# A layer norm behind the experts: its factor applied by the transposing product, its shift laid into PSUM first, the second token tile's sums in another order

## The chip, the cores and the metric

The kernel runs on one core of a Trainium2 chip. Its time is the device time of one execution in microseconds (us). The engines are named as in the profile: PE is TensorE (matmuls and transposes), PEld its weight loads, DVE VectorE, ACT ScalarE, POOL GpSimd, SP the engine that issues most DMAs. They run side by side and meet only in semaphores.

## The reference, cut to what matters

Two blocks stand one behind the other: two layers of mixer, norm, expert layer, norm (256 tokens of 1024 features), and then one recurrent/retention layer with a feed-forward part. The change touches what lies between an expert layer and the projection behind it:

```python
def layer_norm(x, g, b):
    mu = jnp.mean(xf, axis=-1, keepdims=True)
    var = jnp.mean(jnp.square(xf - mu), axis=-1, keepdims=True)
    y = (xf - mu) * lax.rsqrt(var + LN_EPS) * g + b

for i in range(DEPTH):                       # DEPTH = 2
    m = even_mixer(...) if i % 2 == 0 else odd_mixer(...)
    x = layer_norm(DN_ALPHA * x + m, ln1_g[i], ln1_b[i])
    f = hier_moe(x, ...)                     # 32 experts, the best two of one group
    x = layer_norm(DN_ALPHA * x + f, ln2_g[i], ln2_b[i])     # this norm

q, k, v = jnp.split(x @ w_qkv, 3, axis=-1)   # reads it behind the experts of layer 0
proj = rms_norm_2(x, norm1_gain) @ w_in      # reads it behind the experts of layer 1
```

## The kernel before, in words

Every engine has a program of its own, written out by hand in the order in which it runs; nothing is scheduled by rules. The 256 tokens are two tiles of 128 (t = 0, 1), the 1024 features eight columns of 128 (c = 0 to 7). The stretch that the change touches comes twice, once behind the experts of layer 0 and once behind those of layer 1. The two are called **junction 1** (592 to 612 us in the profile) and **junction 2** (1182 to 1205 us).

At a junction PE has added the last pair of experts into PSUM banks 0 to 3 (`scatter_by_half`, L1029). DVE takes the statistics of a tile (`expert_stats`, L1881 and L1885), ACT the root of the variance (`norm_root`, L1489), and DVE makes (x - mean) * gain by halves (`expert_center`, L1907), then the reciprocal of the root (L1865) and x * factor + shift over the whole tile (`norm_scale`, L1891). The shift is the second row of LNR, which holds gain and shift on all 128 partitions. Only then is X ready, and PE transposes its eight 128x128 blocks (`transposes_by_token`, L778) into two PSUM banks.

The projection behind it works with a split of each operand in a high part (rounded to fp32r) and a low part (what is left): high*high, high*low and low*high, called HH, HL and LH in `normed_and_first_chunk`. ACT copies the high part of the input out of the transposes' banks (`high_input`, L1466; with a gain per feature eight small ACTIVATEs per tile, L1469, at junction 2), DVE makes the low part (`low_input`, L1842, at junction 2 L1845). The weights come in quarter tiles of 128x1024: ACT makes the high part (`high_tiles`, L1597), POOL the low part (`low_tiles`, L666), and the first four of them belong to the first chunk of 512 columns. `normed_and_first_chunk` computes that chunk: 24 products per token tile (8 columns, three kinds; L798), then the next chunks follow in `split_project_t` (L916), which waits for `w_lo`, the count of low tiles. A high tile of the next chunk may be written when PE has used the same buffer (`w_used`).

`keep_clock` (L950) are products whose results nobody reads; PE runs them while it would wait. Before the change five of them stand ahead of the branch that leads around the overflow rounds of the experts (`pe.If(more > 0)`), and two behind the first tile's transposes. Products of plain f32 are two records each in the trace, each with a weight load of its own; transposes and fp32r products are one record.

At junction 2 ACT also takes squares of the finished X (`rms_root`, L1497 and L1501), and DVE makes a diagonal of its inverse roots (L2294) that PE sums by columns (L1322) ahead of the second chunk. In ACT's program `rms_root` stands between `high_input` of tile 1 and the first high tile of the second chunk.

## Time and profile before

| what | value |
|---|---|
| time, median of 3 runs | 1523.52 us (1520.9 to 1523.73) |
| time of the profiled execution | 1520.87 us |
| its span in the trace | 1519.1 us |
| granted TensorE clock over the span | 0.998 |
| PE busy | 1471.6 us, 97% |
| DVE, ACT, POOL busy | 552.5, 466.8, 153.8 us |
| chain that ended last, by engine | PE 87%, DMA 5%, DVE 4%, ACT 2% |
| HBM | 500.40 MB read, 330 GB/s over the span |

A row of the timeline gives start, duration, engine, line, operation, output and inputs, shape, and in brackets how long the engine sat idle before and what ended that. Rows of one kind that touch are merged ("x8"), so a pitch from one product to the next is read from two starts. A matmul's duration is longer than its pitch, since products overlap.

### The profile page before, as it was taken

The page shows a single profiled execution, that of the slowest core. Times are in us where ns is not written, and L with a number is a line of the kernel's source. Part 1 is how long each engine was busy: PE and PEld are TensorE (multiplying, and loading weights), DVE is VectorE, ACT ScalarE, POOL GpSimd, SP SyncE. Part 2 cuts the span into 40 slices and gives each one's busy share as a digit, 9 for nine tenths or more (in the row PEclk, how much of TensorE's full clock was granted, in tenths as well). Part 3 has the DMA queues.
Part 4 walks back from the last instruction along what each step waited for, and adds up shares of the span by engine and source line. Part 5 has one row for each costly group of instructions (what it writes and reads, how often), then busy time and mean ns, then how long its engine had stood idle before and what let it go on. Part 6 is the DMA issues. An engine that isn't in the chain of part 4 may idle for free.

```text
span 1519.1 us, 19195 instructions
## 1 busy us (share of the span) xinstructions
PE 1471.6 (97%) x7726; PEld 879.3 (58%) x7726; DVE 552.5 (36%) x1151; ACT 466.8 (31%) x819; POOL 153.8 (10%) x126
## 2 busy tenths in 40 slices
PE   8989999999999999999999999999999999999998
PEld 7755454544544444977544545445444786788886
DVE  6645111111111114037321111211111487688965
ACT  4541111111111113456111111111111561577654
POOL 0211000000000002953100000000000610001200
PEclk9999999999999999999999999999999999999999
DMA  8655999999999999835899999999999846464410
GB/s 300 249 222 221 373 424 427 428 428 427 428 426 428 428 423 398 301 145 238 330 411 426 428 426 428 427 428 428 428 426 409 322 177 220 168 214 174 170 53 28
DMA packets 76228, 502.68 MB, mean 331 GB/s; under 512 B 4720, under 2 KB 6000, under 8 KB 49136
## 3 DMA queue, kind: packets, MB, share of 16 engines
q1 hardware_dynamic: 75280, 495.18, 79.9%
q0 software_dynamic: 864, 6.29, 1.0%
q8 instruction: 64, 1.05, 0.3%
q14 instruction: 20, 0.16, 0.0%
HBM read 500.40 MB, written 1.05 MB: 330 GB/s over the span
## 4 chain that ended last, share of the span: by engine, by line
PE 87%; DMA 5%; DVE 4%; ACT 2%; issue 1%; SPq 1%; POOL 0%; DVEq 0%; ACTq 0%
PE bank L1057 26%; PE bank L1090 14%; PE bank L916 9%; PE bank L1003 7%; PE bank L1374 6%; DMA ring<-in_w_up 4%; PE bank L1402 4%; PE bank L863 4%; PE bank L1017 3%; PE bank L1376 3%; PE bank L882 1%; PE bank L950 1%; PE bank L798 1%; SPq L606 1%; PE bank L1072 1%
## 5 line engine op out<-in xcount | busy, mean ns | idle before, releaser
L1057 PE MATMUL bank<-ring,arena 128*64 128x512 f32 x1280 | 284.2, 599 | 12.0 <-issue 6.8
L1057 PEld LDWEIGHTS bank<-ring,arena 128*64 128x64 f32 x1280 | 94.4, 138 | 196.8 <-issue 192.7
L1057 PE MATMUL bank<-arena 128*64 128x512 f32 x576 | 168.3, 592 | 3.5 <-issue 3.5
L2037 DVE TENSOR_TENSOR arena<-arena,bank 128x512 f32<-128x512 f32 x32 | 22.0, 688 | 383.0 <-PE bank L1057 383.0
L1090 PE MATMUL bank<-ring,arena 128*64 128x512 f32 x640 | 141.7, 595 | 2.4 <-ACT arena L1556 2.4
L1374 PE MATMUL bank<-x_split,w_high 128*128 128x512 f32 (+1 forms) x408 | 139.1, 392 | 0.2 <-DVE x_split L1845 0.2
L1003 PEld LDWEIGHTS bank<-SEL,x_by_row 128*128 128x128 f32 x1024 | 116.7, 192 | 25.8 <-issue 24.3
L1003 PE MATMUL bank<-SEL,x_by_row 128*128 128x128 f32 x1024 | 122.8, 278 | 0.0
L2051 DVE SCALAR_TENSOR_TENSOR y_low<-bank,ST,y_high 128x512 fp32r<-128x512 f32 x64 | 48.1, 751 | 202.4 <-ACT y_high L1560 202.4
L1560 ACT ACTIVATE y_high<-bank,ST 128x512 fp32r<-128x512 f32 x64 | 44.0, 687 | 245.6 <-PE bank L1090 245.6
L1057 PEld LDWEIGHTS bank<-arena 128*64 128x64 f32 x576 | 55.3, 137 | 110.7 <-issue 110.7
L1376 PE MATMUL bank<-x_split,w_low 128*128 128x256 f32 (+1 forms) x408 | 111.8, 274 | 0.0
L2403 DVE TENSOR_TENSOR w_low<-ring,w_high 128x1024 fp32r<-128x1024 f32 x72 | 96.7, 1345 | 30.8 <-ACT w_high L1754 30.6
L1553 ACT COPY arena<-bank 128x512 f32<-128x512 f32 x30 | 17.6, 586 | 262.7 <-PE bank L1003 262.7
L1090 PEld LDWEIGHTS bank<-ring,arena 128*64 128x64 f32 x640 | 45.9, 137 | 84.3 <-issue 84.3
L658 POOL DMA_DIRECT2D LNR<-in_ln_rows x6 | 3.8, 631 | 879.2 <-PE bank L1003 828.6
L1374 PEld LDWEIGHTS bank<-x_split,w_high 128*128 128x128 f32 x408 | 76.7, 188 | 17.5 <-DVE x_split L1845 0.3
L1090 PE MATMUL bank<-arena 128*64 128x512 f32 x288 | 85.0, 595 | 0.0
L1057 PE MATMUL bank<-first_over_features,arena 128*64 128x512 f32 x192 | 84.5, 593 | 0.0
L1754 ACT CAST w_high<-ring 128x1024 fp32r<-128x1024 f32 x72 | 75.5, 1051 | 25.9 <-PE bank L1402 25.9
L1376 PEld LDWEIGHTS bank<-x_split,w_low 128*128 128x128 f32 x408 | 77.2, 189 | 0.2 <-issue 0.2
L1547 ACT ACTIVATE arena<-bank 128x512 f32<-128x512 f32 x32 | 19.1, 598 | 156.9 <-PE bank L1057 156.9
(352 smaller groups left out, 2247.3 us busy)
## 6 DMA issues: line engine op xcount, KB each, us to landing
ring<-in_w_gate SPq DMA_DIRECT2D x32, 2048.0 KB, 27.2
ring<-in_w_up SPq DMA_DIRECT2D x32, 2048.0 KB, 22.5
ring<-in_w_down SPq DMA_DIRECT2D x32, 2048.0 KB, 24.3
arena<-in_w_gate SPq DMA_DIRECT2D x18, 2048.0 KB, 24.2
arena<-in_w_up SPq DMA_DIRECT2D x18, 2048.0 KB, 24.5
arena<-in_w_down SPq DMA_DIRECT2D x18, 2048.0 KB, 25.9
ring<-in_ffn_up SPq DMA_DIRECT2D x12, 2048.0 KB, 8.8
ring<-in_w_in SPq DMA_DIRECT2D x8, 2048.0 KB, 13.6
```

The lines of the kernel that those rows point to most:

```text
L863: last = nc.tensor.matmul(bank[(g0 + n) % 2 * 2 + t][:, :], tile(c, t), slot(i[n], C, 512)[:, c, :], start=(c == first), stop=(c == final))
L916: last = nc.tensor.matmul(part_(bank[g % 2 * 2 + t]), a, b, start=(part_ is parts[0] and c == 0 and n == 0), stop=(part_ is parts[-1] and ...
L1003: last = nc.tensor.matmul(bank[6 + c // 4][:, c % 4 * P:(c % 4 + 1) * P], x_rows(t, c), SEL[:, t, :], start=(t == 0), stop=(t == T - 1))
L1017: last = nc.tensor.matmul(bank[2 * t + half][:, :], SWT[:, t, :], y[:, 512 * half:512 * half + 512], start=False, stop=False, skip_group_c ...
L1057: last = nc.tensor.matmul(bank[4 + m][64 * e:64 * e + 64, :], XG[:, c, 64 * e:64 * e + 64], w[e][:, c, :], start=(c == 0), stop=(c == C - 1))
L1090: last = nc.tensor.matmul(bank[6 + half][64 * e:64 * e + 64, :], HT[:, j, 64 * e:64 * e + 64], w[e][:, j, 512 * half:512 * half + 512], st ...
L1374: nc.tensor.matmul(bank[f % 4][:, :].rearrange("p (a b) -> p a b", a=2)[:, :, a:b], WHI[f % WBUF][:, c, :], XSPLIT[:, :, c, a:b], start=(a ...
L1376: last = nc.tensor.matmul(bank[f % 4][:, a:b], WLO[f % WBUF][:, c, :], XHI[:, c, a:b], start=False, stop=(b == SEQ and c == C - 1), skip_g ...
L1402: last = nc.tensor.matmul(bank[4 + 2 * t + half][:, :], a, w.rearrange("p a b -> p (a b)"), start=(c == 0 and n == 0), stop=(c == DOWN_T - ...
L1754: nc.scalar.copy(WHI[k % WBUF][:, :, :], src).then_inc(w_hi, 1)
L2051: v.scalar_tensor_tensor(YLO[:, cols_], bank[6 + half][:, :], slot_gate, YHI[:, cols_].bitcast(F32), ALU.mult, ALU.subtract).then_inc(s["y ...
L2403: v.tensor_tensor(WLO[k % WBUF][:, :, :], ffn_weights(k)[1], WHI[k % WBUF][:, :, :], ALU.subtract)\
```

## The change

The factor 1/sqrt(var) of a token no longer has to be in X before the transposes. A transpose is a product with the identity; with a diagonal matrix in its place the same product scales each token as it transposes. ACT makes that matrix (`make_diagonal`: identity times the token's factor) in the buffer of SELW, which is free by then. The shift, which is a number per feature, is laid into the same PSUM blocks first by a product of LNR's second row with the first column of the identity, repeated 128 times (`shift_by_token`); `scaled_transposes` then adds onto it. Both are plain f32 products, where the transposes were moves.

X itself is finished by DVE later, behind both `low_input`s. The reciprocal stands between the two halves of `expert_center`. POOL no longer waits for X before its first low tile, and ACT begins with a high tile ahead of the first root. PE has two `keep_clock` products ahead of the branch and none behind it, and the sums of tile 1 are reordered: HH and HL of the first two weight tiles, then their LH, then the same for tiles 2 and 3.

```diff
         SEL, SELW = sb("SEL", [P, T, 2 * SLOTS]), sb("SELW", [P, T, 2 * SLOTS])
+        NORM_DIAG = SELW
         bank = [ctx.enter_context(nc.psum_tensor(f"bank{i}", [P, 512], F32)) for i in range(8)]
...
+        x_prepared, diag_made = sem("x_prepared"), sem("norm_diagonal_made")
...
             next_norm_rows(0, 1)
-            pool.wait_ge(x_ready, 3)
             low_tiles(S_QKV, range(3 * TILES))
             pool.wait_ge(x_ready, 4)
...
             next_norm_rows(1, 3)
-            pool.wait_ge(x_ready, 7)
             low_tiles(S_IN2, range(3 * TILES))
...
-            def normed_and_first_chunk(name, source, ready, n0, s, after):
+            def normed_and_first_chunk(name, l, s):
 
                 g, width = s["g0"], s["widths"][0]
                 HH, HL, LH = (XHI, 0), (XHI, 1), (XLO, 0)
@@ -798,15 +798,41 @@
                             last = nc.tensor.matmul(bank[g % 2 * 2 + t][:, 0:width], x[:, c, t * P:(t + 1) * P],
                                                     s["bufs"][q][half][:, c % 2, 0:width],
                                                     start=(kind is HH and c == 0),
-                                                    stop=(c == C - 1 and kind is kinds[-1] and kind is not HH and
-                                                          (t == 1 or kind is HL)))
+                                                    stop=(c == C - 1 and kind is (LH if t else HL)))
                     return last
 
                 def x_high(t, half):
                     pe.wait_ge((tr_act, tr_dve)[half], TR[name][0] // 2 + t + 1)
 
-                transposes_by_token(name, source, ready, n0, [0])
-                keep_clock(7, after)
+                def norm_blocks(t):
+
+                    for h in range(2):
+                        k = TR[name][0] + 2 * t + h
+                        pe.wait_ge(tr_dve if k % 2 else tr_act, (k - 4) // 2 + 1)
+                        for j in range(4):
+                            c = 4 * h + j
+                            yield h, j, bank[4 + k % 4][:, j * P:(j + 1) * P], slice(c * P, (c + 1) * P)
+
+                def shift_by_token(t):
+
+                    pe.wait_ge(ln_loaded, 16 * (2 * l + 2))
+                    for h, j, block, features in norm_blocks(t):
+                        nc.tensor.matmul(block, LNR[:, 1, features], ident[:, 0:1].broadcast_to([P, P]),
+                                         start=(j == 0), stop=False, skip_group_check=True)
+
+                def scaled_transposes(t):
+
+                    pe.wait_ge(diag_made, 2 * l + t + 1)
+                    pe.wait_ge(x_prepared, 4 * l + 2 * t + 2)
+                    for h, j, block, features in norm_blocks(t):
+                        last = nc.tensor.matmul(block, X[:, t, features], NORM_DIAG[:, t, :], start=False, stop=(j == 3),
+                                                skip_group_check=True)
+                        if j == 3:
+                            last.then_inc(tr_done, 1)
+
+                shift_by_token(0)
+                scaled_transposes(0)
+                shift_by_token(1)
                 pe.wait_ge(pj_free[0], g - 1)
                 for q in range(TILES):
                     if q % 2 == 0:
@@ -816,21 +842,27 @@
                 for q in range(TILES // 2):
                     pe.wait_ge(w_lo, s["k0"] + q + 1)
                     products(0, q, [HL])
-                transposes_by_token(name, source, ready, n0, [1])
+                scaled_transposes(1)
                 pe.wait_ge(x_lo, s["x0"] + 2)
                 for q in range(TILES):
                     products(0, q, [LH])
                 for half in range(2):
                     x_high(1, half)
-                pe.wait_ge(x_lo, s["x0"] + 4)
                 pe.wait_ge(pj_free[1], g - 1)
-                for q in range(TILES):
+                for q in range(TILES // 2):
+                    products(1, q, [HH, HL])
+                pe.wait_ge(x_lo, s["x0"] + 3)
+                for q in range(TILES // 2):
+                    products(1, q, [LH]).then_inc(w_used, 1)
+                for q in range(TILES // 2, TILES):
                     pe.wait_ge(w_lo, s["k0"] + q + 1)
-                    if q >= TILES // 2:
-                        last = products(0, q, [HL])
-                        if q == TILES - 1:
-                            last.then_inc(pj_done, 1)
-                    products(1, q, [HH, HL, LH]).then_inc(*((w_used, 1) if q < TILES - 1 else (pj_done, 1)))
+                    last = products(0, q, [HL])
+                    if q == TILES - 1:
+                        last.then_inc(pj_done, 1)
+                    products(1, q, [HH, HL])
+                    pe.wait_ge(x_lo, s["x0"] + 4)
+                    products(1, q, [LH]).then_inc(*((w_used, 1) if q < TILES - 1 else (pj_done, 1)))
...
                 scatter_by_half(n)
-                keep_clock(7, 5)
+                keep_clock(7, 2)
...
-            normed_and_first_chunk("ln1", X, x_ready, 2, S_QKV, 2)
+            normed_and_first_chunk("ln1", 0, S_QKV)
...
-            normed_and_first_chunk("n1", X, x_ready, 6, S_IN2, 2)
+            normed_and_first_chunk("n1", 1, S_IN2)
...
+            def make_diagonal(l, t):
+
+                act.wait_ge(x_prepared, 4 * l + 2 * t + 1)
+                nc.scalar.activation(NORM_DIAG[:, t, :], ident, ACT.Copy, scale=rs_l[:, t:t + 1]).then_inc(diag_made, 1)
+
+            def high_input(name, t, gain=None, halves=range(2)):
+
+                for h in halves:
+                    copied = (tr_act, tr_dve)[h]
                     k = TR[name][0] + 2 * t + h
                     act.wait_ge(tr_done, k + 1)
...
-            for t in range(T):
-                norm_root(t)
-                if t == 0:
-                    high_tiles(S_QKV, range(TILES))
-                high_input("ln1", t)
+            def norm_by_features(l, name, s, gain=None):
+
+                high_tiles(s, [0])
+                norm_root(0)
+                high_tiles(s, [1])
+                make_diagonal(l, 0)
+                high_tiles(s, [2])
+                high_input(name, 0, gain, [0])
+                norm_root(1)
+                high_input(name, 0, gain, [1])
+                make_diagonal(l, 1)
+                high_tiles(s, [3])
+                high_input(name, 1, gain)
+
+            norm_by_features(0, "ln1", S_QKV)
             for n in range(6):
                 dest = (OQ if n < 3 else OK)[:, 4 * ((n - 1) % 2):4 * ((n - 1) % 2) + 2, :] if 0 < n < 5 else \
                     OV[:, 0, 512 * (n // 5):512 * (n // 5) + 512]
@@ -1696,12 +1744,7 @@
...
-            norm_root(0)
-            high_tiles(S_IN2, range(3))
-            high_input("n1", 0, Q_N1)
-            norm_root(1)
-            high_tiles(S_IN2, range(3, TILES))
-            high_input("n1", 1, Q_N1)
+            norm_by_features(1, "n1", S_IN2, Q_N1)
...
                 for n in range(2):
                     half = slice(512 * n, 512 * n + 512)
+                    if n:
+                        dve.wait_ge(std_ready, roots[0])
+                        v.reciprocal(rs_l[:, t:t + 1], var_l[:, t:t + 1]).then_inc(x_prepared, 1)
                     last = v.scalar_tensor_tensor(X[:, t, half], bank[2 * t + n][:, :], mv[:, t, 0:1], LNR[:, 0, half],
                                                   ALU.subtract, ALU.mult)
-                link(last)
+                last.then_inc(x_prepared, 1)
+
+            def norm_by_features(l, name, gain=None):
+
+                for t in range(T):
+                    expert_stats(l, t)
+                    expert_center(l, t)
+                for t in range(T):
+                    low_input(name, t, gain)
+                for t in range(T):
+                    dve.wait_ge(tr_done, TR[name][0] + 2 * t + 2)
+                    dve.wait_ge(x_prepared, 4 * l + 2 * t + 2)
+                    v.scalar_tensor_tensor(X[:, t, :], X[:, t, :], rs_l[:, t:t + 1], LNR[:, 1, :], ALU.mult, ALU.add)\
+                        .then_inc(x_ready, 1)
 
             def mixed_norm(l, g0, name, copy_first=True):
 
...
             moe_layer(0)
-            expert_stats(0, 0)
-            expert_center(0, 0)
-            norm_scale(0)
-            expert_stats(0, 1)
-            expert_center(0, 1)
-            norm_scale(1)
-            low_input("ln1", 0)
-            low_input("ln1", 1)
+            norm_by_features(0, "ln1")
...
             moe_layer(1)
-            expert_stats(1, 0)
-            expert_center(1, 0)
-            norm_scale(0)
-            expert_stats(1, 1)
-            expert_center(1, 1)
-            norm_scale(1)
-            low_input("n1", 0, Q_N1)
-            low_input("n1", 1, Q_N1)
+            norm_by_features(1, "n1", Q_N1)
```

PE, from the end of the branch at junction 1, before. KT is the table with the identity, "qkv_high" and "x_split" are the split weights and the split input:

```order
L1191 UNCONDITIONAL_BRANCH
L778 MATMUL bank<-KT,X 128x128 [waits tr_act,x_ready]
L778 MATMUL bank<-KT,X 128x128 x3
L778 MATMUL bank<-KT,X 128x128 [waits tr_dve]
L778 MATMUL bank<-KT,X 128x128 x3
L950 MATMUL bank<-KT 128x512 x2
```

The same place now:

```order
L1223 UNCONDITIONAL_BRANCH
L820 MATMUL bank<-KT,LNR 128x128 [waits tr_act,ln_loaded]
L820 MATMUL bank<-KT,LNR 128x128 x3
L820 MATMUL bank<-KT,LNR 128x128 [waits tr_dve]
L820 MATMUL bank<-KT,LNR 128x128 x3
L828 MATMUL bank<-SELW,X 128x128 [waits tr_act,x_prepared,norm_diagonal_made]
L828 MATMUL bank<-SELW,X 128x128 x3
L828 MATMUL bank<-SELW,X 128x128 [waits tr_dve]
L828 MATMUL bank<-SELW,X 128x128 x3
L820 MATMUL bank<-KT,LNR 128x128 [waits tr_act,ln_loaded]
L820 MATMUL bank<-KT,LNR 128x128 x3
L820 MATMUL bank<-KT,LNR 128x128 [waits tr_dve]
```

Eight transposes and two clock products became 24 f32 products (the last four of the second shift follow), and X's finish is no longer waited for.

ACT, from the end of its own branch at junction 1, before. "ST" holds the small statistics:

```order
L1581 UNCONDITIONAL_BRANCH
L1489 ACT_TABLE_LOAD
L1489 ACTIVATE ST<-ST 128x1 [waits var_ready]
L1597 CAST qkv_high_83<-ring 128x1024 [waits moe_gate_done,slot_loaded0]
L1597 CAST qkv_high_85<-ring 128x1024 [waits moe_gate_done,slot_loaded0]
```

And now:

```order
L1619 UNCONDITIONAL_BRANCH
L1635 ACT_TABLE_LOAD [waits moe_gate_done]
L1635 CAST qkv_high_83<-ring 128x1024 [waits slot_loaded0]
L1527 ACT_TABLE_LOAD
L1527 ACTIVATE ST<-ST 128x1 [waits var_ready]
L1635 CAST qkv_high_85<-ring 128x1024 [waits moe_gate_done,slot_loaded0]
L1494 ACTIVATE SELW<-KT,ST 128x128 [waits x_prepared]
```

The moved high tile brought a table load of its own, and the root keeps the one that it had: two loads and a cast now stand ahead of the first root. It is the same at junction 2.

DVE at junction 2, from the second tile's centring on, before:

```order
L1907 SCALAR_TENSOR_TENSOR X<-bank,ST,LNR 128x512
L1865 RECIPROCAL ST<-ST 128x1 [waits std_ready,dve_step]
L1891 SCALAR_TENSOR_TENSOR X<-X,ST,LNR 128x1024 [waits dve_step]
L1845 SCALAR_TENSOR_TENSOR x_split<-bank,COLS,x_split 128x128 [waits tr_act]
L1845 SCALAR_TENSOR_TENSOR x_split<-bank,COLS,x_split 128x128 x3
```

And now, with the last four of the 16 operations that make the input's low parts:

```order
L1888 SCALAR_TENSOR_TENSOR x_split<-bank,COLS,x_split 128x128 [waits tr_dve]
L1888 SCALAR_TENSOR_TENSOR x_split<-bank,COLS,x_split 128x128 x3
L1967 SCALAR_TENSOR_TENSOR X<-X,ST,LNR 128x1024 [waits x_prepared,tr_done] x2
L1908 RECIPROCAL ST<-ST 128x1 [waits std_ready]
L1908 RECIPROCAL ST<-ST 128x1 [waits std_ready,dve_step]
```

X's two finishing operations moved from ahead of the low parts to behind them.

## Rows read from the trace of the kernel before

**Rows 1.** Page, part 1: busy us (share of the span) and instructions.

```profile
PE 1471.6 (97%) x7726; PEld 879.3 (58%) x7726; DVE 552.5 (36%) x1151; ACT 466.8 (31%) x819; POOL 153.8 (10%) x126
```

**Rows 2.** Chain of waits, 575 to 760 us: start, us, what.

```profile
599.68 2.74 DVE X L1891
...
603.68 8.45 PE bank L798 x36
```

**Rows 3.** Timeline of PE, junction 1: start, us, engine, line, operation.

```profile
592.68 4.46 PE L950 MATMUL bank<-KT 128*128 128x512 f32 x10
596.98 1.04 PE L778 MATMUL bank<-KT,X 128*128 128x128 f32 x8
597.85 1.88 PE L950 MATMUL bank<-KT 128*128 128x512 f32 x4
...
611.97 0.40 PE L916 MATMUL bank<-x_split,qkv_high 128*128 128x256 f32 x2
```

**Rows 4.** Timeline of PE, the gather for a pair of experts: 16 plain f32 products.

```profile
550.12 3.84 PE L1003 MATMUL bank<-SEL,x_by_row 128*128 128x128 f32 x32
553.79 0.38 PE L1072 MATMUL bank<-KT,arena 128*128 128x128 f32 x2
```

**Rows 5.** Timeline of ACT, junction 1.

```profile
591.29 1.28 ACT L1489 ACT_TABLE_LOAD   x1
593.63 0.29 ACT L1489 ACTIVATE ST<-ST 128x1 f32<-128x1 f32 x1 [1.05 <-DVE ST L1885]
593.83 3.87 ACT L1597 CAST qkv_high<-ring 128x1024 fp32r<-128x1024 f32 x4
```

**Rows 6.** Timeline of ACT, two table loads with work waiting behind them.

```profile
1228.22 1.28 ACT L1720 ACT_TABLE_LOAD   x1
1229.52 1.15 ACT L1720 ACTIVATE arena<-arena 128x512 f32<-128x512 f32 x2
```

**Rows 7.** Line L536, SP's DMA issues, 560 to 600 us.

```profile
L536 SPq DMA_DIRECT2D ring<-in_w_qkv x4: 368/1370/2644, 580.2 to 591.0; - x4
...
DMA to landing us min/median/max: 11.9/14.8/17.7
```

**Rows 8.** Timeline of DVE, junction 1.

```profile
591.31 0.75 DVE L2051 SCALAR_TENSOR_TENSOR y_low<-bank,ST,y_high 128x512 fp32r<-128x512 f32 x1 [0.90 <-ACT y_high L1560]
591.98 1.37 DVE L1881 BATCH_NORM_STATS2 ST<-bank 128x6 f32<-128x512 f32 x2
...
593.63 1.41 DVE L1907 SCALAR_TENSOR_TENSOR X<-bank,ST,LNR 128x512 f32<-128x512 f32 x2
...
595.27 1.28 DVE L1891 SCALAR_TENSOR_TENSOR X<-X,ST,LNR 128x1024 f32<-128x1024 f32 x1
```

**Rows 9.** Timeline of all engines, junction 2.

```profile
1186.82 10.38 POOL L666 TENSOR_TENSOR in_low<-ring,in_high 128x1024 fp32r<-128x1024 f32 x4 [42.01 <-DVE X L1891]
...
1192.53 4.21 DVE L1845 SCALAR_TENSOR_TENSOR x_split<-bank,COLS,x_split 128x128 fp32r<-128x128 f32 x16
...
1192.66 1.09 PE L778 MATMUL bank<-KT,X 128*128 128x128 f32 x8
1193.36 2.18 ACT L1469 ACTIVATE x_split<-bank,COLS 128x128 fp32r<-128x128 f32 x8 [2.28 <-PE bank L778]
...
1195.37 1.11 ACT L1497 ACTIVATE arena<-X 128x1024 f32<-128x1024 f32 x1
...
1196.81 1.04 ACT L1497 ACTIVATE arena<-X 128x1024 f32<-128x1024 f32 x1
...
1197.97 0.29 ACT L1501 ACTIVATE ST<-ST 128x1 f32<-128x1 f32 x1
...
1199.80 14.22 POOL L666 TENSOR_TENSOR in_low<-ring,in_high 128x1024 fp32r<-128x1024 f32 x6 [2.61 <-ACT in_high L1597]
...
1203.42 0.60 PE L1322 MATMUL bank<-arena,KT 128*128 128x128 f32 x4
...
1203.79 0.48 PE L916 MATMUL bank<-x_split,in_high 128*128 128x256 f32 x2
```

2 lines of the change are left out of this document (removed).

## The prediction

> **What bounds the kernel now.** I read the page first. PE is busy 97% of the span [rows 1], so a change counts as far as it moves PE. It touches two stretches, junction 1 and junction 2, and everything behind each of them waits for PE. The chain of waits shows how junction 1 ends: DVE finishes X, and then 36 products of L798 follow without a gap [rows 2]. The timelines of PE, ACT and DVE then show who is late for whom. PE starts the first transposes at 596.98, when its five clock products are through, and the second chunk (L916) at 611.97 [rows 3]; X was finished at 596.55 [rows 8]. So the path through a junction has three parts: ACT's root and DVE's X until 596.6, then PE's own products, and inside them a gap before the second transposes, since X of tile 1 takes 2.74 us instead of 1.28 and ends at 602.4 [rows 2, 8].
>
> I take L916's start as the end of a junction. Junction 2 is the same program 590.2 us later: X's finish plus 0.1 us is 596.65 at junction 1, and POOL starts there at 1186.82 [rows 8, 9].
>
> **Price of the new products.** The transposes take 0.87 us for eight (596.98 to 597.85) [rows 3]. They become plain f32 products, 128x128 on 128 columns. The trace has that form in the gather: 16 products from 550.12 to the next kind at 553.79, 3.67 us, so 0.23 us each and 1.84 us for eight [rows 4]. The two products of L1322 are the other nearest rows, from 1203.42 to 1203.79, 0.185 each [rows 9]. That pair is too short to be a pitch, so I take 0.23 and keep 0.185 for the range. The shift's products have the same form with another moving operand. There are four groups of eight per junction, 7.36 us, where before there were two groups of transposes, 1.74 us. What goes is five clock products per junction: five took 592.68 to 596.98, 0.86 each, so 4.3 us [rows 3]. PE has 1.3 us more to do per junction, and its gaps must pay for that.
>
> **When the scaled transposes may start, junction 1.** Two clock products end at 592.68 + 1.72 = 594.4, and the first shift at 596.24. The diagonal comes from ACT. The order of the changed kernel puts two table loads ahead of the first root, one for the moved high tile and one for the root. The load starts at 591.29 and takes 1.28; four casts take 3.87, so 0.97 each; the root takes effect 0.2 before the next cast and is 0.29 long [rows 5]. So: load to 592.57, cast to 593.6, load to 594.9, root to 595.2, cast of tile 1 from 595.1 to 596.1, diagonal (an eighth of 2.18, 0.27 [rows 9]) to 596.4. Before, the root ran at 593.63, when its variance came [rows 5]: it is now 1.3 us late. DVE's reciprocal then falls at 595.3 and the second half of the centring (half of 1.41 [rows 8]) ends at 596.15, earlier than the diagonal. PE starts at **596.45**, where before it started at 596.98.
>
> The moved cast needs its ring tile at 592.6. SP's first issue is at 580.2, and the shortest way to landing is 11.9 [rows 7]: 592.1, so it is there, with 0.5 us of cover.
>
> A rule of the Trainium skill speaks here. Loads with work queued behind them show no more than their own length: 1228.22 plus 1.28 is 1229.50, and the next operation starts at 1229.52 [rows 6]. The Trainium skill ("ScalarE: Activation LUTs", What ACT_TABLE_LOAD costs) states about 1283 ns for the load, which the trace has, and a drain of about 1380 ns on top, which these rows don't have. By the page the first root would start some 2.8 us later and the sum would be about 5.5 us more; that is a rival below, priced there from rows.
>
> **The rest of junction 1 on PE.** From 596.45: 1.84 (scaled transposes), 1.84 (second shift), 12 products of HH and HL, 1.84 (tile 1's transposes), 36 products. The 36 took 8.29 us (603.68 to 611.97) [rows 2, 3], 0.23 each, so the 12 take 2.76. The sum is 16.57 and the end 613.0, against 611.97: **+1.05 us**. The old gap before the second transposes is gone, as X is no longer waited for: tile 1's centring ends near 599.6 (statistics, root, reciprocal as before, 1.1 us later), its diagonal too, and PE needs them at 602.9. Cover is 3.3 us. Cast 3 is done near 600.6 and wanted at 601.6. POOL starts its low tiles at 593.6 instead of 596.65 and delivers tiles 1 and 2 by 601.5 at 2.6 each (10.38 for four [rows 9]); wanted at 602.1. The first low tile of the next chunk is tighter: its high tile waits for tile 1's LH of the first weight tile, which the new order puts behind eight other products (608.8), then cast 1.0 and POOL 2.4 (14.22 for six [rows 9]) give 612.4 where PE is ready at 613.0. Costed at nothing; 0.6 us of cover. If POOL slows DVE's centring as it did X's finish (2.74 for 1.28), up to 0.5 us is added, since POOL now runs beside it.
>
> **Junction 2.** PE's sum is the same: 1186.62 + 16.57 = 1203.2 at L1322, against 1203.42, so -0.2: here the gap before was longer. But DVE finishes X behind all low parts, and ACT's squares of X stand ahead of the first high tile of the next chunk. Step by step: tile 1's scaled transposes start at 1186.62 + 1.84 + 1.84 + 2.76 = 1193.06. ACT began 0.70 after the transposes did (1192.66, 1193.36), with four of them (0.43) in it; four f32 products are 0.92, so ACT begins at 1194.25 and is through after 2.18, at 1196.4. DVE's last quarter of the low parts (4.21 for 16, so 1.05 for four) ends at 1197.5. X is finished at 1198.8 and 1200.1, 1.28 each since POOL is idle then. The squares begin 1.44 apart (1195.37, 1196.81) and the last root 1.16 behind the second (1197.97) [rows 9]: 1198.8, 1200.25, 1201.4. The cast follows 0.2 later and takes 1.0: 1202.6. POOL's tile takes 2.37: 1205.0. PE's L916 waits for that tile and starts at 1205.1 instead of 1203.79: **+1.3 us**. Before, POOL had begun this tile at 1199.80, the cast having needed only `w_used`. So a wait takes the place of the one removed, on `w_lo`, and behind it stands the whole rest of PE's program. L1322 needs the diagonal of the inverse roots near 1202.5 and gets it in time.
>
> Both stretches pass to the end: behind junction 1 the chunks are PE's without a gap, and the second layer's expert loads wait for buffers that PE frees. The sum is 1.05 + 1.3 = **+2.35 us**: the profiled execution, 1520.87 us (span 1519.1 plus 1.8 around it), would be 1523.2. It lies 2.65 below the median of the runs, 1523.52, so the forecast for a median is **1525.9 us**.
>
> **Rivals.**
>
> *Intended gain, 8%.* PE starts earlier, X is off the path, and the products cost 0.185. Junction 1 is then 1.05 - 3 x 0.36 = 0.0. If the low tile is also in time, junction 2 is -0.2 - 1.1 = -1.3: 1522.2 us. For it speaks the freed gap; against it that POOL's tile cannot start before ACT's squares.
>
> *Products cheap, wait stays, 20%.* Junction 1 at 0.0 and junction 2 at 1.3 - 0.9 = 0.4: 1523.9 us.
>
> *A branch that is no longer covered, 15%: slower.* PE's branch around the overflow rounds had 4.3 us of clock products in its queue and now has 1.7. On DVE a branch at the same point hid behind an operation of 0.75 us (591.31, next start 591.98) [rows 8], but PE's jump is the longest. It decides from 1.9 us on (1.7 plus the 0.2 that PE waits for the diagonal) and costs at most 4.3 - 1.9 = 2.4 per junction, since before no delay is seen: up to 1525.9 + 4.8 = 1530.7, with the middle at 1528.3. The Trainium skill ("Runtime: NRT & Kernel Launch", Instruction fetch mechanics) says that a taken branch out of the fetched window stalls for a fetch; no row here shows that on PE.
>
> *Table loads that hold ACT twice as long, 2%: slower.* Two more times 1.28 us ahead of the first root at both junctions, so 1525.9 + 5.1 = 1531.0; [rows 6] speak against it. It is what the Trainium skill's rule above comes to.
>
> The forecast itself holds the other 55%, from 1524.5 to 1527.5: the diagonal 0.3 us off at each junction, 0.5 of DVE beside POOL, 0.3 in the expert phase.
>
> **How the numbers follow.** About 0.2%, 3.0 us, is what a measurement of this kernel can tell from no change. 1525.9 is +0.16%. Slower than 0.2% takes in both slow rivals (17%) and the forecast's upper end with the scatter of the runs (15%): 32%. Faster by 0.2% needs 1520.5, which only the intended gain and scatter can give: 6%. The rest is 62%. The range reaches from the intended gain, 1522.3, to the branch's middle and a little over, 1529.0.
>
> **What would show it.** In the changed trace: 16 records of L820 or L828 in about 1.84 us; two ACT_TABLE_LOADs and a cast between 591.3 and 594.9, the root at 594.9; PE's first L828 at 596.5, with an idle time of 0.2 put down to ACT; no gap before the second L828; L948 at 613.0; at junction 2 L1354's products (the old L1322) at 1203 and then PE idle for some 1.4 us until POOL's low tile. It is wrong if eight products take under 1.5 us, if PE sits idle between the clock products and the first L820, or if that last idle time isn't there.

## The result

The changed kernel takes 1527.88 us (median of 10 runs, 1525.35 to 1530.75). The kernel before, run beside it on the same chip, takes 1521.75 us (1518.97 to 1524.08). The ratio is 1.0037, with a 95% interval of 1.0027 to 1.0047: the change makes the kernel 0.37% slower, 5.6 us by the ratio and 6.1 us by the two medians. The profiled execution of the changed kernel took 1527.48 us, its span is 1525.7 us, and the span before was 1519.1, so 6.6 us are to be found in the two traces.

The page's first part answers [rows 1]. PE is busy 3.4 us more, in 76 more matmul records, and idle 3.2 us more.

```profile
PE 1475.0 (97%) x7802; PEld 888.2 (58%) x7802; DVE 550.8 (36%) x1151; ACT 470.7 (31%) x825; POOL 151.7 (10%) x126
```

**Where they are.** I measure a junction from the first instruction behind the scatter's last product to the first product of the second chunk (L916 before, L948 after). Before, that was 611.97 - 592.68 = 19.29 us at junction 1 [rows 3] and 1203.79 - 1182.85 = 20.94 us at junction 2 [rows 9]. Here is PE at junction 1 of the changed kernel (timeline: start, us, engine, line, operation, and in brackets the idle time ahead of it and what ended it). It answers [rows 3]; L820 are the shift's products, L828 the scaled transposes, and everything lies 0.95 us later than before.

```profile
593.63 1.88 PE L982 MATMUL bank<-KT 128*128 128x512 f32 x4
595.35 1.95 PE L820 MATMUL bank<-KT,LNR 128*128 128x128 f32 x16
597.48 0.60 PE L828 MATMUL bank<-SELW,X 128*128 128x128 f32 x3 [0.18 <-ACT SELW L1494]
599.92 1.72 PE L828 MATMUL bank<-SELW,X 128*128 128x128 f32 x13 [1.84 <-issue]
...
606.02 1.95 PE L828 MATMUL bank<-SELW,X 128*128 128x128 f32 x16
...
615.98 0.40 PE L948 MATMUL bank<-x_split,qkv_high 128*128 128x256 f32 x2
```

The junction takes 22.35 us, 3.06 more than before. From the start of a group of eight products (16 records) to the start of the next it is 1.7 to 1.9 us, so the price of the new products was right. But the fourth line was in nobody's sum: after three records of the scaled transposes PE stops, and what ended the stop is "issue", which means that the profile shows nothing that PE waited for. 599.92 - 597.48 is 2.44 us for three records that need 0.32 (0.107 each), so the break costs 2.12 us (1.84 of it is shown as idle).

ACT at the same place (answers [rows 5]): two table loads with a cast between them, the root at 595.89, which is 594.94 in the times of before, and the diagonal.

```profile
592.24 1.28 ACT L1635 ACT_TABLE_LOAD   x1
593.53 1.04 ACT L1635 CAST qkv_high<-ring 128x1024 fp32r<-128x1024 f32 x1
594.60 1.28 ACT L1527 ACT_TABLE_LOAD   x1
595.89 0.29 ACT L1527 ACTIVATE ST<-ST 128x1 f32<-128x1 f32 x1
...
597.03 0.40 ACT L1494 ACTIVATE SELW<-KT,ST 128x128 f32<-128x128 f32 x1
```

Junction 2 takes 1209.37 - 1186.37 = 23.00 us, 2.06 more than before. PE, ACT and POOL in its timeline (answers [rows 9], 3.52 us later than there):

```profile
1186.37 1.88 PE L982 MATMUL bank<-KT 128*128 128x512 f32 x4
...
1186.53 1.04 ACT L1635 CAST in_high<-ring 128x1024 fp32r<-128x1024 f32 x1 [0.28 <-DMA ring<-in_w_in]
...
1190.47 1.94 PE L828 MATMUL bank<-SELW,X 128*128 128x128 f32 x15 [0.45 <-ACT SELW L1494]
...
1192.65 0.38 PE L828 MATMUL bank<-SELW,X 128*128 128x128 f32 x1 [0.24 <-issue]
...
1203.08 1.06 ACT L1535 ACTIVATE arena<-X 128x1024 f32<-128x1024 f32 x1 [2.38 <-DVE X L1967]
...
1205.83 2.92 ACT L1635 CAST in_high<-ring 128x1024 fp32r<-128x1024 f32 x3
...
1206.94 9.46 POOL L668 TENSOR_TENSOR in_low<-ring,in_high 128x1024 fp32r<-128x1024 f32 x4 [9.04 <-ACT in_high L1635]
...
1209.37 0.50 PE L948 MATMUL bank<-x_split,in_high 128*128 128x256 f32 x2 [1.37 <-POOL in_low L668]
```

The last four lines are the chain of the forecast: X's finish, the squares, the cast of the next chunk's first high tile, POOL's low tile, and PE waits 1.37 us for it. The first lines add two small things: the ring's tile was 0.28 us late for the moved cast, and a short break of the same kind (the 15 records took 2.18 us to the next one instead of 1.61) stands here after 15 records.

The account of the 6.6 us: junction 1 +3.06, junction 2 +2.06, and between and around them +0.95 (ahead of junction 1), -0.49 (between), +1.02 (behind junction 2; there PE waits 2.5 us for DVE's low tiles, before it was 1.8). Ahead of junction 1 nothing was changed in PE's program but the numbers of its lines, and PE's idle time there is even 0.3 us shorter. What differs is the granted clock: the changed kernel's profile has a stretch of 3.41 us at 0.50, from 73.52 us on, where the profile before has 1.00 (the line: length of the stretch; busy time of PE, PEld, DVE, ACT and POOL; granted clock; DMA share; GB/s). So one profile can differ by a microsecond without the change, and the reading below goes by the lengths of the junctions.

```profile
73.52:76.93 3.41, 3.41 (x18) 3.33 (x18) 0.69 (x3) 1.55 (x5) 0.00 (x0) 0.50 1.02 432
```

### The profile page after: what moved, and what is told of

It reads as the page before. It is cut to its first block, busy times and chain, and to the rows that moved or that the text cites. A ratio compares the mean times of both kernels' runs of the same rounds, so it can differ in the third digit from the quotient of the medians.

```text
span 1525.7 us, 19353 instructions
## 1 busy us (share of the span) xinstructions
PE 1475.0 (97%) x7802; PEld 888.2 (58%) x7802; DVE 550.8 (36%) x1151; ACT 470.7 (31%) x825; POOL 151.7 (10%) x126
## 3 DMA queue, kind: packets, MB, share of 16 engines
q0 software_dynamic: 864, 6.29, 1.0%
HBM read 500.40 MB, written 1.05 MB: 329 GB/s over the span
## 4 chain that ended last, share of the span: by engine, by line
PE 87%; DMA 6%; DVE 3%; ACT 2%; issue 1%; SPq 1%; POOL 0%; DVEq 0%; ACTq 0%
PE bank L1089 26%; PE bank L1122 13%; PE bank L948 9%; PE bank L1035 7%; PE bank L1406 6%; DMA ring<-in_w_up 4%; PE bank L1434 4%; PE bank L895 4%; PE bank L1049 3%; PE bank L1408 3%; PE bank L914 1%; PE bank L798 1%; SPq L608 1%; PE bank L1104 1%; DMA ring<-in_w_in 1%
```

## The experiments

Twelve kernels ran. The question was what the break is, since it is most of what the sum lacked. My theory: PE's instructions come in pieces from memory, and behind the branch around the overflow rounds PE runs dry, for which the clock products had been the cover. Rivals: a property of the scaled transposes (the diagonal, PSUM), the clock products as real work on the path, the low tile's wait, the table loads, and the order of the sums. This table has the lengths of both junctions in every profile, measured as above, and the break at junction 1: when PE goes on, counted from the scatter's end, which is the start of the first instruction behind it. (At junction 2 of clock_behind PE is idle for 0.40 us ahead of that instruction; the 0.40 is in its length.)

| kernel | median us | ratio to before (95%) | junction 1 | junction 2 | PE goes on at |
|---|---|---|---|---|---|
| before | 1521.5 to 1522.7 | | 19.29 | 20.94 | no break |
| changed | 1527.88 | 1.0037 (1.0027 to 1.0047) | 22.35 | 23.00 | 6.29 |
| clock5 | 1530.79 | 1.0057 (1.0040 to 1.0075) | 22.45 | 24.36 | no break |
| clock_behind | 1527.65 | 1.0038 (1.0024 to 1.0052) | 21.85 | 22.74 | 5.78 |
| clock0 | 1527.15 | 1.0033 (1.0021 to 1.0045) | 24.29 | 22.18 | 5.80 |
| before_clock2 | 1524.81 | 1.0027 (1.0018 to 1.0036) | 19.32 | 23.45 | no break |
| no_shift | 1524.02 | 1.0016 (1.0006 to 1.0026) | 21.24 | 22.11 | no break |
| tile4_early | 1529.98 | 1.0048 (1.0032 to 1.0064) | 22.04 | 24.91 | 5.98 |
| tile4_first | 1527.52 | 1.0034 (1.0020 to 1.0049) | 22.00 | 22.58 | 5.96 |
| one_table | 1530.49 | 1.0061 (1.0045 to 1.0077) | 21.85 | 22.50 | 5.79 |
| code_shifted | 1535.51 | 1.0087 (1.0073 to 1.0102) | 25.41 | 27.63 | 5.89 |
| old_sums | 1530.44 | 1.0053 (1.0034 to 1.0072) | 22.39 | 27.48 | 6.30 |
| before_new_sums | 1524.82 | 1.0012 (1.0003 to 1.0021) | 20.89 | 22.18 | no break |
| combined | 1528.31 | 1.0037 (1.0023 to 1.0050) | 19.86 | 22.92 | no break |

### More clock products ahead of the branch: clock5

```diff
-                keep_clock(7, 2)
+                keep_clock(7, 5)
```

> The changed kernel with five clock products ahead of the branch behind the experts instead of two. Theory A (PE's next instructions are still on their way when it comes out of the branch, and the clock products were the time in which they came): the break of 1.84 us inside the scaled transposes of the first junction goes, 2.6 us of clock products come, so the first junction ends about 0.7 us later; at the second the 2.6 us eat the 1.37 us wait for the low tile, so it ends about 1.0 us later; 1529.6 us in all. Theory B (the fetch is asked for only behind the branch, so what stands ahead of it is no cover): the break stays, 2.6 us later, and the first junction ends 2.6 us later; 1531.5 us. Theory C (the break is the two SELW diagonals or PSUM, nothing of the supply): as B in time, but the break moves or goes without any change of the instruction DMA's place.

PE at junction 1 (timeline):

```profile
596.52 4.45 PE L982 MATMUL bank<-KT 128*128 128x512 f32 x10
600.81 2.02 PE L820 MATMUL bank<-KT,LNR 128*128 128x128 f32 x16
602.66 1.95 PE L828 MATMUL bank<-SELW,X 128*128 128x128 f32 x16
```

No break, at either junction. That is theory A's outcome: time ahead of the branch is cover. The scaled transposes by themselves have nothing in them that breaks (theory C). The three more clock products cost 2.57 us, what went with the break and the wait for the diagonal is 2.47 by difference, and junction 1 is as long as it was, within 0.1 us. At junction 2 I was wrong on one point: I had the low tile's wait eaten by the clock products, but it stayed at 1.37 us to the hundredth. POOL's tile hangs on ACT's squares, these on X, X on the transposes, and those on PE: the chain that PE waits for starts at PE itself, so delaying PE delays it as well.

### The clock products moved behind the branch: clock_behind

```diff
-                keep_clock(7, 2)
                 with pe.If(more > 0):
...
                 shift_by_token(0)
+                keep_clock(7, 2)
                 scaled_transposes(0)
```

> The changed kernel with its two clock products put behind the branch, between the first shift products and the first scaled transposes. The same work in another order. Theory A (instructions are still on their way behind the branch): the clock products, few instructions that last long, now stand where the short products ran dry, so the 1.84 us break shrinks to 0.2 us or less if the fetch runs from the branch on; 1526.1 us. Theory B (the fetch started by what PE has consumed, wherever it stands): the break keeps its size and sits at another product; 1527.9 us. Either way the 0.18 and 0.45 us waits for the diagonal are no longer than now.

```profile
593.77 2.02 PE L820 MATMUL bank<-KT,LNR 128*128 128x128 f32 x16
595.63 1.88 PE L983 MATMUL bank<-KT 128*128 128x512 f32 x4
597.53 0.60 PE L828 MATMUL bank<-SELW,X 128*128 128x128 f32 x3
599.55 1.72 PE L828 MATMUL bank<-SELW,X 128*128 128x128 f32 x13 [1.42 <-issue]
```

Neither prediction: the break stays behind the same record, and PE goes on 5.78 us after the scatter instead of 6.29. It is a matter of both a place and a time. The place is an instruction: as many instructions stand ahead of the third record of L828 as in the changed kernel, since the clock products went from one side of the branch to the other and are ahead of it in both. The time is that at which something arrives.

### No clock products: clock0

```diff
-                keep_clock(7, 2)
```

> The changed kernel without the two clock products ahead of the branch behind the experts. The runs so far had PE break off after the third record of the scaled transposes until 5.8 to 6.3 us after the scatter's last product, wherever the clock products stood. Theory A (supply: the block of instructions behind that record arrives at a fixed time after the scatter): the break ends at the same 5.8 to 6.3 us, so it grows from 1.8 to some 3.5 us (part of it now as a wait for the diagonal) and the junction ends where it does now, if the clock holds; behind an idle stretch of this length the run without the shift products showed a granted clock of 0.50, at which the 20 products behind it cost up to 1.6 us more: 0 to +1.6 us per junction, 1527.9 to 1531 us. Theory B (the break has a fixed length, or hangs on how fast PE consumes): the junction ends 1.7 us sooner, 1524.4 us.

Timeline of PE, then the table by stretches (us of a stretch; busy time of PE, PEld, DVE, ACT, POOL; PEclk is the granted clock):

```profile
592.84 2.02 PE L820 MATMUL bank<-KT,LNR 128*128 128x128 f32 x16
596.61 1.05 PE L828 MATMUL bank<-SELW,X 128*128 128x128 f32 x7 [1.75 <-ACT SELW L1493]
598.64 2.29 PE L828 MATMUL bank<-SELW,X 128*128 128x128 f32 x9 [0.98 <-issue]
600.72 3.62 PE L820 MATMUL bank<-KT,LNR 128*128 128x128 f32 x16
```

```profile
599.00:601.00 2.00, 2.00 (x11) 2.00 (x11) 0.93 (x3) 0.81 (x3) 2.00 (x1) 0.50 1.04 384
601.00:603.00 2.00, 2.00 (x11) 2.00 (x11) 1.17 (x2) 1.78 (x3) 0.14 (x2) 0.50 1.06 389
```

The break has moved from the third to the seventh record. Four records are missing ahead of it, so it stands at the same instruction of the program, 8 instructions having gone (a record is a weight load and a matmul). And it ends 5.80 us after the scatter, with 1.7 us less work in front: the end is fixed, as theory A says. Behind it the granted clock is 0.50, that is 1.2 GHz instead of 2.4: a group of 16 records takes 3.62 us instead of 1.95, and the junction is 1.9 us longer. Junction 2 has no break here at all and is 0.8 us shorter, which is why the total is no worse.

### The same on the kernel before: before_clock2

```diff
-                keep_clock(7, 5)
+                keep_clock(7, 2)
```

> The kernel before with two clock products instead of five ahead of the branch behind the experts, all else as before. Theory A (these products only fill the time in which PE waits for the norm of the first token and for its instructions): the transposes of the first token wait up to 2.6 us longer, the junction ends where it did, and only a lower granted clock behind the idle time can cost, 0 to 1 us per junction: 1521.6 to 1523.6 us. Theory B (they were work on the path, the 2.6 us per junction that the change set out to use): 1516.4 us.

At junction 1 theory A holds to 0.03 us: the transposes wait 2.05 us for DVE's X and the junction keeps its length. At junction 2 it is otherwise:

```profile
1181.22 1.88 PE L950 MATMUL bank<-KT 128*128 128x512 f32 x4
1186.98 1.94 PE L778 MATMUL bank<-KT,X 128*128 128x128 f32 x8 [3.88 <-issue]
```

PE stands 3.88 us right behind the branch, until 5.76 us after the scatter, and the transposes then run at a granted clock of 0.50. The clock products were no idle filler: taking them away costs 2.5 us at this junction in a kernel in which nothing else is changed. The median is 3.3 us above the kernel before; the profiled execution itself is the fastest of the twelve (1519.93), so the 2.5 us rest on the junction's length and not on its total. Whether it is their 2.6 us as cover or the 24 instructions by which the program has become shorter up to here, this run doesn't tell; the next one shows that the second can do it alone.

### The place in the program: code_shifted

```diff
                 with pe.If(more > 0):
                     s = over[l]
                     pe.drain().then_inc(over_free[l], 1)
+                    keep_clock(7, (18, 8)[l])
```

> The changed kernel with clock products added inside the branch that is never taken (18 behind the first experts, 8 behind the second): nothing more is executed, but what follows lies 72 and 104 instructions further on in PE's program. Theory A (PE is supplied in blocks of 16384 B, and the break is the edge of a block that stands 11 products behind the branch at the first junction and 31 records behind it at the second): both edges move in front of the branch's end and the next ones stand over 200 instructions later, so the 1.84 us break goes and the 0.24 us one too: 2.1 us less, 1525.8 us. Theory B (the break belongs to the scaled transposes, PSUM or the diagonal, or to a time after the scatter and not to a place in the program): it stays, 1527.9 us. A third outcome, that the edge now makes PE wait at the branch itself, would cost up to 3.9 us, as at the second junction of the kernel before with two clock products.

```profile
592.61 1.88 PE L982 MATMUL bank<-KT 128*128 128x512 f32 x4
598.50 3.40 PE L820 MATMUL bank<-KT,LNR 128*128 128x128 f32 x16 [4.00 <-issue]
```

and the DMA queues from 592.6 to 598.5 (packets, MB, share):

```profile
q8 instruction: 1, 0.02, 1.2%
```

This is the third outcome, and the clearest run. Not one instruction more is executed, but the program is 72 and 104 instructions further on behind the branches, and the whole is 1.0087 times as long as before. The break has gone from its record, to the branch's target, at both junctions (4.00 and 3.97 us), and ends 5.89 and 5.85 us after the scatter.

With this the mechanism is clear, but for one point that `combined` leaves open below. The records of queue 8 are instruction DMAs of 16384 B. The Trainium skill ("Runtime: NRT & Kernel Launch", Instruction fetch mechanics) says that instructions are refilled in blocks of 16 KiB, 256 instructions, and that a taken branch whose target lies outside the two blocks held makes the engine wait for a fetch. The traces agree with it and add the times.

Counted in the built programs, the branch of the changed kernel jumps some 370 instructions, into the block next to its own. That one is there, and PE runs to its end, the record at which it breaks. The count gives the same instruction for the break at junction 1 in the changed kernel, clock_behind, clock0, tile4_early, one_table and old_sums, and the short break at junction 2 of the changed kernel stands a whole multiple of 256 behind it. With 72 instructions more, the target lies one block further, and PE stops at once. In before_clock2 the 24 instructions that are missing up to junction 2 have put the branch ahead of an edge behind which it stood, and its target there is two blocks on as well. The kernel before has such an edge too: at junction 1 it lies, by the count, 13 records behind the target. Eight transposes and two clock products are 12 of them, and PE starts the next products (L798) at 599.17, 6.5 us after the scatter, when the block had come: its DMA landed at 597.22. In clock5 the 12 instructions more put the edge at the same record; PE reaches it near 602.3 (an estimate, 13 records of 0.115 us from 600.81), 5.8 us after the scatter, and doesn't stop.

```profile
599.17 2.38 PE L798 MATMUL bank<-qkv_high,x_split 128*128 128x512 f32 x8
```

Why the end is a fixed time can be read as well. At junction 1 the instruction DMA starts 3.2 to 3.9 us after the scatter's end in all fourteen profiles, 3.27 us after it without any clock products (clock0) and 3.28 with five (clock5). So the clock products do not delay the fetch, and their time passes beside it.

In the six cases of this table PE goes on 1.3 to 1.7 us after the landing; in the other breaks at such an edge it is 1.2 to 1.5 us.

| kernel, junction | instruction DMA starts | lands | PE goes on | later by |
|---|---|---|---|---|
| changed, 1 | 597.51 | 598.60 | 599.92 | 1.32 |
| clock_behind, 1 | 597.05 | 598.22 | 599.55 | 1.33 |
| clock0, 1 | 596.11 | 597.29 | 598.64 | 1.35 |
| code_shifted, 1 | 595.82 | 596.94 | 598.50 | 1.56 |
| code_shifted, 2 | 1191.16 | 1192.21 | 1193.91 | 1.70 |
| before_clock2, 2 | 1184.33 | 1185.46 | 1186.98 | 1.52 |

### Without the shift's products: no_shift

```diff
-                shift_by_token(0)
                 scaled_transposes(0)
-                shift_by_token(1)
```
with `start=(j == 0)` in the scaled transposes.

> The changed kernel without the shift products (the norm's shift is left out of the transposed copy, so the projections behind it are computed without it; X itself keeps it). 32 products of 0.23 us fewer, 7.4 us by themselves. Ahead of the first token they covered the wait for the diagonal (ready 2.1 us after PE comes out of the branch), so only those of the second token can be saved: 1.8 us per junction, at the second of which the low tile's wait eats 1.4 us. If the 1.84 us break is instructions on their way, it passes inside the wait for the diagonal: 1527.9 - 1.8 - 1.8 - 0.5 = 1523.7 us. If it is not, it stays: 1525.5 us.

This kernel leaves out the norm's shift in the transposed copy. Its median is 1524.02 against the 1523.7 of the supply theory. PE waits 2.47 us for the diagonal, inside which the fetch passes, and then runs at the lower clock:

```profile
592.88 1.88 PE L980 MATMUL bank<-KT 128*128 128x512 f32 x4
597.23 3.50 PE L828 MATMUL bank<-SELW,X 128*128 128x128 f32 x16 [2.47 <-ACT SELW L1492]
```

```profile
599.00:601.00 2.00, 2.00 (x11) 1.90 (x10) 1.15 (x4) 1.01 (x3) 2.00 (x2) 0.50 1.06 390
```

Even without 32 of the 64 new products the junctions are 1.95 and 1.17 us longer than before. That the total came out close owes something to chance: the junctions give back 2.0 us, the rest of the 3.9 lies elsewhere in the program.

### The next chunk's first high tile sooner: tile4_early and tile4_first

In tile4_early ACT casts it between the two squares of X, in tile4_first ahead of both.

```diff
             rms_root(0, XN, x_ready, 7)
+            high_tiles(S_IN2, [TILES])
             rms_root(1, XN, x_ready, 8)
```

> The changed kernel with ACT casting the next chunk's first high tile at the second junction between the two squares of the norm that follows, instead of behind both. Forecast's reason (the wait of 1.37 us at the first low product of that chunk is POOL held by this cast): POOL starts 1.4 us sooner, the wait goes, 1.4 us less, 1526.5 us. Rival (the low tile itself, 2.4 us each on POOL, is the bound for the whole chunk, or ACT's buffer is free only later): the wait moves to the chunk's later tiles, 1527.9 us.

Junction 2 of tile4_early (timelines of POOL, DVE and PE):

```profile
1207.22 7.03 POOL L668 TENSOR_TENSOR in_low<-ring,in_high 128x1024 fp32r<-128x1024 f32 x3 [7.65 <-ACT in_high L1635]
...
1208.82 3.18 DVE L2342 TENSOR_SCALAR arena<-KT,ST 128x128 f32<-128x128 f32 x2
...
1212.06 1.22 PE L1354 MATMUL bank<-arena,KT 128*128 128x128 f32 x4 [2.87 <-DVE arena L2342]
```

The low tile's wait is gone and a longer one has come: DVE's two small scalings, 0.48 us in the changed kernel, take 3.18 us while POOL runs, and PE waits 2.87 us for them and falls to half its clock. Neither theory had it. POOL's first tiles end near 1209.6 and 1211.9; DVE's second scaling ends at 1212.0.

> The changed kernel with ACT casting the next chunk's first high tile at the second junction ahead of both squares, in the time in which it is idle (2.4 us) until X is finished. With the cast between the squares, POOL's low tile ran beside DVE's two scalings of the diagonals, which took 3.18 us instead of 0.48, and PE waited 2.87 us for them. Theory A (DVE's operations between buffers in SBUF run slower while POOL computes): POOL's first tile now ends before the diagonals but falls on DVE's finish of X (two of 1.24 us), which takes up to 2 us longer, and PE waits for the diagonal instead of the low tile, 0 to +1 us: 1527.9 to 1529 us. Theory B (it was the order alone): the wait for the low tile of 1.37 us goes, 1526.5 us.

```profile
1204.54 2.40 POOL L668 TENSOR_TENSOR in_low<-ring,in_high 128x1024 fp32r<-128x1024 f32 x1 [6.45 <-ACT in_high L1635]
...
1207.51 0.48 DVE L2342 TENSOR_SCALAR arena<-KT,ST 128x128 f32<-128x128 f32 x2
...
1208.05 0.71 PE L1354 MATMUL bank<-arena,KT 128*128 128x128 f32 x4 [0.64 <-DVE arena L2342]
```

Here POOL's tile is over before the scalings come, and these take 0.48 again. The wait for the low tile (1.37) has become one for the diagonals (0.64), and junction 2 is 0.42 us shorter although its scaled transposes started 0.8 us later than in the changed kernel. DVE's finish of X did not suffer as theory A had it, for the buffer came free only at 1203.4, and POOL began when X was done.

### One table load ahead of the root: one_table

```diff
-                high_tiles(s, [0])
                 norm_root(0)
-                high_tiles(s, [1])
+                high_tiles(s, [0])
+                high_tiles(s, [1])
```

> The changed kernel with ACT taking the first root ahead of the ring's first high tile, so that only one table load stands between the experts and the root instead of two and a cast. The diagonal is ready 2.3 us sooner; PE's waits for it (0.18 and 0.45 us) go. Forecast's reading (the break behind it belongs to something else): the break takes up what is gained at the first junction, since its end is fixed, and 0.2 to 0.4 us are gained at the second: 1527.5 us. Rival (the root is what sets the first junction's end): 2 us per junction less, 1523.9 us.

```profile
594.89 0.57 PE L828 MATMUL bank<-SELW,X 128*128 128x128 f32 x3
597.18 1.72 PE L828 MATMUL bank<-SELW,X 128*128 128x128 f32 x13 [1.72 <-issue]
```

PE no longer waits for the diagonal, and the break takes it up: it ends 5.79 us after the scatter. Each junction is 0.5 us shorter. I had the diagonal 2.3 us sooner, and it is 0.4 (3.03 us after the scatter instead of 3.40), since two casts now stand between the root and the diagonal. The median says the opposite of the junctions, 2.6 us more than the changed kernel; its profiled execution, with a span of 1522.8 us, is the fastest of its six (1524.6 to 1533.4). What lengthens the others no profile shows; for effects of half a microsecond the totals here are no evidence.

### The order of the sums: old_sums and before_new_sums

In old_sums the changed kernel has tile 1's sums in the order of before; in before_new_sums the kernel before has the new order, and POOL does not wait for X (two edits; the wait read below stands ahead of all the sums, so it belongs to the second).

> The changed kernel with tile 1's sums of the first chunk in the order of before (each quarter's three kinds together, all of them behind the last low part of X). Forecast's reading: the low parts come some 3 us before they are needed in the new order, so the old one makes PE wait for them, 0.5 to 1.5 us per junction, and the ring's tiles come free later: 1529 to 1531 us. Rival (the order moves nothing, since DVE's low parts are early enough): 1527.9 us.

From the second group of L828 to L948 junction 1 takes 9.98 us, and 9.96 in the changed kernel; at junction 2 it is 11.96 against 11.94, with 0.9 us more waiting inside and 1.1 less for the low tile. So the new order is worth nothing, and the forecast of 0.5 to 1.5 us was wrong. What makes this kernel's junction 2 so long is again the supply, here in two places:

```profile
1188.75 2.02 PE L820 MATMUL bank<-KT,LNR 128*128 128x128 f32 x16 [1.54 <-issue]
...
1194.65 0.58 PE L828 MATMUL bank<-SELW,X 128*128 128x128 f32 x2 [2.31 <-issue]
```

They follow instruction DMAs that landed at 1187.28 and 1193.21, 1.47 and 1.44 us earlier. The second of them started 6.00 us behind the first, so a first one that comes late makes the next one late as well: PE goes on behind the edge 9.32 us after the scatter.

> The kernel before with the new order of tile 1's sums and without POOL's wait for X ahead of the low tiles: what the change moves, without what it does to the norm. Forecast's reading: PE is idle 0.13 us at the first junction and 1.1 us at the second, so 0 to 0.5 us can be gained: 1521.2 us; POOL's earlier start beside DVE's norm costs at most 0.5 us per junction. Rival (POOL beside DVE's operations between SBUF buffers holds the norm, as it held the diagonals by 2.7 us): 1.2 to 2.7 us per junction more, up to 1526.9 us.

The rival was right:

```profile
594.96 11.33 POOL L666 TENSOR_TENSOR qkv_low<-ring,qkv_high 128x1024 fp32r<-128x1024 f32 x4 [37.10 <-ACT qkv_high L1599]
...
595.28 3.11 DVE L1893 SCALAR_TENSOR_TENSOR X<-X,ST,LNR 128x1024 f32<-128x1024 f32 x1
...
598.45 1.09 PE L776 MATMUL bank<-KT,X 128*128 128x128 f32 x8 [1.30 <-DVE X L1893]
```

X's finish took 1.28 us before [rows 8]; with POOL running it takes 3.11, and PE waits 1.30 us for it at both junctions, which are 1.6 and 1.2 us longer. POOL's wait for X, which the change could drop since X's finish had left the path, was what kept POOL away from DVE. The Trainium skill ("SBUF — State Buffer", SBUF: two separate sides) says that DVE and GpSimd share a pair of ports as an exclusive lock: whichever starts first has it for the whole instruction, and the other is blocked, where DVE's operation has two inputs in SBUF or runs in a two-port mode. These rows agree with it: POOL's first tile ends at 597.32, and X's finish 1.08 us later, where alone it takes 1.28.

### The edge moved to a harmless place: combined

```diff
-            keep_clock(3, 3)
...
-                        keep_clock(6, 1)
+                        keep_clock(6, l)
...
-                        keep_clock(5, 1)
+                        keep_clock(5, l)
...
-                keep_clock(5, 4)
+                keep_clock(5, 4 * l)
...
-                keep_clock(5, 1)
+                keep_clock(5, l)
```
together with the edits of one_table and tile4_first.

> The changed kernel with three edits: ten clock products of the start and of the first layer's router left out (seven ahead of its experts, three at the kernel's start; 40 instructions of PE's program), ACT's first root ahead of the ring's first tile, and the next chunk's first high tile ahead of the squares at the second junction. Supply theory with its numbers from the runs so far: at the first junction the block's edge stands 44 instructions behind the branch's target (the break began at records 20, 24 and 24 of the changed kernel, the one without and the one with moved clock products, always the same instruction), a place in code that is two blocks on makes PE wait at the branch itself, and what lies beyond the edge comes 5.85 us after the scatter. 40 instructions fewer put the edge at record 40, which PE reaches 6.3 us after the scatter: no break at the first junction (now 1.84 us), none at the second. First junction 2.0 us shorter, second 1.5 us shorter (the low tile's wait 1.37 less, up to 0.6 for the diagonal), 1524.4 us; up to 3 us more where the left out clock products let the granted clock fall ahead of the router and the gather. Rival (the break is a time after the scatter and not a place in the program): a break of 1.8 us at the first junction, at or behind record 16.

```profile
598.65 1.88 PE L982 MATMUL bank<-KT 128*128 128x512 f32 x4
600.37 1.95 PE L820 MATMUL bank<-KT,LNR 128*128 128x128 f32 x16
602.15 2.02 PE L828 MATMUL bank<-SELW,X 128*128 128x128 f32 x16
```

This was the test of the theory by its own numbers, and at junction 1 it holds: ten clock products were left out, all of them far ahead of it, at the start and around the first router, and the break is gone. Junction 1 takes 19.86 us, 2.49 less than in the changed kernel and 0.57 more than before. At junction 2 it failed. There is a break of another kind:

```profile
1194.32 2.02 PE L820 MATMUL bank<-KT,LNR 128*128 128x128 f32 x16 [1.62 <-issue]
```

It stands at the branch's target, which by the count lies in the block next to the branch's own, and it ends 3.5 us after the scatter, not 5.85; the instruction DMA of 16384 B that comes 1.53 us ahead of it had started only 0.74 us after the scatter's end. The first break of old_sums is the same. At junction 2 of clock_behind, with no clock products in front, PE is idle for 0.40 us at the target, until 1.53 us behind a landing. Why the next block is in hand in some cases and not in others stays open. What the traces show apart in combined and old_sums is when the block's fetch began: 0.74 and 0.77 us after the scatter's end, where in the changed kernel, which has no break at the target, it was 2.03 us ahead of that end. The left out clock products had their price. Up to junction 1 PE's idle time is 6.6 us longer than in the changed kernel, and the granted clock is 0.50 from 143.21 to 146.62 and from 150.04 to 156.87, where it is 1.00 in the changed kernel; the total, 1528.31, is no gain.

No version tried beats the kernel before.

## Why the prediction was near, and where it failed

The forecast was +2.35 us and 1525.9; the measured 1527.88 lies in its range, and the sign of the difference was right. Part of that nearness is luck. The forecast was added to 1523.52, the median of three runs, where ten runs of the kernel before give 1521.75. Against that base the difference is 6.1 us, 2.6 times the +2.35, and in the two traces it is 6.6. The 4.25 us that the sum lacks in the traces are 2.01 at junction 1 (one mechanism, which stood among the rivals), 0.76 of small terms at junction 2, and 1.48 outside the junctions, where the sum had nothing.

- **Price of the new products: right.** 1.7 to 1.8 us from one group of eight to the next; 0.23 us each was the right row, 0.185 would have been too low.
- **Start of the scaled transposes: right.** Forecast 596.45 with 0.2 us of waiting for ACT; 597.48 - 0.95 = 596.53 with 0.18. Two table loads and a cast stood ahead of the root, as read from the order, the root at 594.94 instead of 594.9. The diagonal took 0.40 us, not 0.27: an eighth of a run of eight is the pitch, not the duration of a single one.
- **Table loads: right.** 594.60 plus 1.28 is 595.88, and the root starts at 595.89. The drain that the Trainium skill ("ScalarE: Activation LUTs", What ACT_TABLE_LOAD costs) puts on top isn't there; the rival of 1531.0 us falls.
- **Rest of junction 1: the sum was right, the supply was missing.** Forecast 16.57 us from the first scaled transpose; measured 18.50, of which 2.12 are the break, so 16.38 without it. The term that failed is +1.05 for the junction, which was 3.06. In its own steps: 1.05 + 0.08 (start) + 2.12 (break) - 0.19. The prediction costed the clock products at their time on PE and put their other work, covering the branch, into a rival with 15%.
- **That rival: right in kind, wrong in place.** It gave 1528.3 us, and 1527.88 came, which is near by luck too, with the base that was 1.8 us too high. It looked for idle time between the clock products and the first L820; there was none in the changed kernel, since the target's block was there. It came where that block ended. "It decides from 1.9 us on" supposed that the wait starts at the branch. What was measured is that PE goes on with the instructions beyond the blocks held 5.8 to 6.3 us after the scatter's end, and once (old_sums, junction 2) only after 9.3.
- **Cover of tile 1 and of the next chunk's low tile at junction 1: right.** No wait stands at the second group of L828 or at L948.
- **POOL beside DVE, up to 0.5 us: not at this place.** DVE's operations that read PSUM (the centring) kept their 0.7 us each with POOL running, and X's finish lies behind POOL's first tiles now. The same neighbours cost 1.8 us where DVE works from SBUF to SBUF (before_new_sums).
- **Junction 2: the wait was right.** Forecast a wait of some 1.4 us for POOL's low tile behind ACT's squares; it is 1.37. The junction came out +2.06 instead of +1.3. The 0.76 more were there at tile 1's transposes already (1193.91 in the times of before instead of 1193.06, 0.85 us): the ring's tile landed 0.28 us late for the cast, the diagonal is 0.13 longer, and the block's edge costs 0.57 here. The cover of 0.5 us for the ring's tile had been worked out for junction 1 alone.

## What to carry to other kernels

Work that seems to fill time on an engine may cover the fetch of its own instructions behind a branch, so before it is taken out, find what stands behind the next branch and where a block of 256 instructions ends; a program can get slower by code that is never run. A wait that orders two engines can also keep them apart: here POOL's wait for X protected a DVE operation from losing 1.8 us. And a wait on a chain that begins at the waiting engine itself is not shortened by giving that engine more to do.
